# The last chunk's hand-over to the down-projection: one split earlier, one load earlier, and the last two groups crossed by tiles

## What is computed

```python
def conv_ffn(h, w_up, conv_w, conv_b, w_down):
    u = causal_dwconv(h @ w_up, conv_w, conv_b)      # width 3
    gate, val = jnp.split(u, 2, axis=-1)             # 2816 columns each
    return (jax.nn.silu(gate) * val) @ w_down        # 2816 -> 1024

for i in range(2):
    ...                                              # mixer, cross-attention, output projection
    x = x + conv_ffn(rms_norm(x, ffn_norm[i]), ffn_w_up[i], ffn_conv_w[i], ffn_conv_b[i], ffn_w_down[i])
```

## Time and profile before

| | before |
|---|---|
| runs, us | 2585.62, 2587.39, 2590.01 (median 2587.39) |
| the profiled execution, us | 2585.62 |
| its span from first to last instruction, us | 2583.8 |
| PE busy | 2489.5 us, 96% |
| DVE, ACT, POOL busy | 60%, 38%, 8% |
| mean granted TensorE clock | 0.986 of full |

### The profile page before, as it was taken

The page is one execution under the profiler, slowest core; times in us unless marked ns, Lnnn a source line. Parts: engine busy times, 40 slices in busy tenths (PEclk is TensorE's granted clock), DMA queues, the critical chain, the costliest instruction groups (busy, mean ns, idle before and its releaser), DMA issues. The chain is left out here.

```text
span 2583.8 us, 32258 instructions
## 1 busy us (share of the span) xinstructions
PE 2489.5 (96%) x11964; PEld 2109.8 (82%) x11964; DVE 1539.9 (60%) x2562; ACT 992.0 (38%) x2000; POOL 196.0 (8%) x269
## 2 busy tenths in 40 slices
PE   7999979999999999998999999998999999999998
PEld 7998767888888878787889889887888888887886
DVE  4432464489999863433553562464779998984332
ACT  6433443344444432423334432333444444443221
POOL 1010020000000000001211021113000000000000
PEclk9999988999999999999999999999999999999999
DMA  4320112222222246442102011212622222226442
GB/s 145 99 75 21 50 66 62 86 67 94 78 90 82 74 163 225 157 146 73 52 17 78 34 33 45 55 33 79 197 86 82 90 82 75 89 90 242 170 159 81
DMA packets 207475, 240.41 MB, mean 93 GB/s; under 512 B 36776, under 2 KB 140184, under 8 KB 207320
## 3 DMA queue, kind: packets, MB, share of 16 engines
q1 hardware_dynamic: 203160, 238.34, 27.8%
q10 hardware_dynamic: 4160, 0.02, 0.1%
HBM read 189.24 MB, written 49.09 MB: 92 GB/s over the span
## 5 line engine op out<-in xcount | busy, mean ns | idle before, releaser
L53 PE MATMUL psum<-f_T_lo,f_up_hi 128*128 128x512 f32 x1024 | 400.7, 391 | 0.0
L52 PE MATMUL psum<-f_T_lo,f_up_hi 128*128 128x512 f32 x704 | 277.8, 395 | 20.9 <-DVE f_up_lo L523 19.4
L54 PE MATMUL psum<-f_T_lo,f_up_lo 128*128 128x512 f32 x704 | 276.1, 392 | 0.0
L518 DVE TENSOR_TENSOR f_T_lo<-h_room_hi,f_T_lo 128x2048 fp32r<-128x2048 f32 x44 | 100.8, 2292 | 261.6 <-ACT f_T_lo L341 261.6
L52 PE MATMUL psum<-w_hi,hT_hi 128*128 128x512 f32 x576 | 229.5, 398 | 4.1 <-DVE w_lo L1224 2.4
L54 PE MATMUL psum<-w_hi,hT_lo 128*128 128x512 f32 x576 | 226.5, 393 | 0.0
L53 PEld LDWEIGHTS psum<-f_T_lo,f_up_hi 128*128 128x128 f32 x1024 | 193.8, 189 | 39.9
L53 PE MATMUL psum<-w_lo,hT_hi 128*128 128x512 f32 x576 | 226.3, 393 | 0.0
L341 ACT ACTIVATE f_T_lo<-h_room_hi 128x2048 fp32r<-128x2048 f32 x44 | 84.3, 1916 | 307.3 <-PE psum L54 276.9
L52 PEld LDWEIGHTS psum<-f_T_lo,f_up_hi 128*128 128x128 f32 x704 | 133.5, 190 | 51.3 <-DVE f_up_lo L523 21.9
L54 PEld LDWEIGHTS psum<-f_T_lo,f_up_lo 128*128 128x128 f32 x704 | 133.4, 189 | 28.0
(11 more groups left out here) (367 smaller groups left out, 5629.2 us busy)
## 6 DMA issues: line engine op xcount, KB each, us to landing
raw<-in_ffn_w_up_dram SPq DMA_DIRECT2D x88, 512.0 KB, 4.6
h_room_hi<-in_ffn_w_down_dram SPq DMA_DIRECT2D x88, 512.0 KB, 4.6
activations<-f_act SPq DMA_DIRECT2D x44, 512.0 KB, 2.6
h_room_lo<-activations SPq DMA_DIRECT2D x44, 512.0 KB, 6.0
w_raw<-in_b_w_in_dram SPq DMA_DIRECT2D x18, 1024.0 KB, 6.2
x_between<-XY SPq DMA_DIRECT2D x16, 512.0 KB, 5.1
XY<-x_between SPq DMA_DIRECT2D x4, 2048.0 KB, 12.1
w_raw<-in_a_w_in_dram SPq DMA_DIRECT2D x8, 768.0 KB, 5.8
```

The costliest lines, as they stand in the source:

```text
L52: nc.tensor.matmul(out, lhs_hi, rhs_hi, start=start, stop=False)
L53: nc.tensor.matmul(out, lhs_hi, rhs_lo, start=False, stop=False)
L54: return nc.tensor.matmul(out, lhs_lo, rhs_hi, start=False, stop=stop)
L518: nc.vector.tensor_tensor(w_lo[s], w_raw[s], w_hi[s].bitcast(F32), ALU.subtract).then_inc(b_split, 1)
```

## The change

Three places in `ffn_phase`, so each acts in f0 and in f1:

- SP issues `load_down(2)` right behind `load_down(1)`, ahead of the store of the last chunk; `begin`'s loads come behind `load_down(3)`, and lose a wait of their own.
- In the last chunk DVE's `low_down(0)` and `low_act(0)` move from behind C21 to behind U3, the step that takes the fourth product, P7; U4, C22 and C21 now come after them.
- PE waits for group 20 alone, multiplies its tiles 6 and 7, and only then waits for group 21; tiles 4 and 5 take both groups as before, tiles 6 and 7 group 21 alone.

```diff
             load_down(1)
+            load_down(2)
             store_act(FC - 1)
-            if begin:
-                sp.wait_ge(op_split, operand(FC - 1, S4))
-                begin.load(sp)
-            for n in range(2, LAST + 1):
+            for n in range(3, LAST + 1):
                 load_down(n)
+                if begin and n == 3:
+                    begin.load(sp)
...
                 mix_step(c, U3)
+                if not more:
+                    low_down(0)
+                    low_act(0)
                 if more:
...
                 mix_step(c, C21)
                 if more:
                     low(c + 1, L22)
-                else:
-                    low_down(0)
-                    low_act(0)
...
+            wait_split(LAST - 1)
+            for t in (6, 7):
+                for half in range(2):
+                    down(LAST - 1, t, half, False, False)
             wait_split(LAST)
             for t in range(4, TT):
                 for half in range(2):
-                    down(LAST - 1, t, half, False, False)
+                    if t < 6:
+                        down(LAST - 1, t, half, False, False)
                     down(LAST, t, half, False, True).then_inc(out_done, 1)
```

## The result

The changed kernel takes 2567.18 us in the median of four executions, beside 2586.51 us for the kernel before on the same chip: a ratio of 0.992, 95% interval 0.990 to 0.994. The forecast was 2566.0 us, its range 2561.5 to 2571.5. In two later comparisons the ratio was 0.990 (0.989 to 0.991) and 0.991 (0.990 to 0.993). The profiled execution takes 2567.03 us, its span is 2565.3 (2583.8 before), PE is busy 2485.6 us, 97%.

What follows compares the result with a forecast made beforehand. PE, busy 96%, bounds the kernel; gains come from its waits and slow-clock matmuls. Terms 9.4 - 0.6 + 7.7 + 4.8 give 21.3 us, so 2566.0 us against the median of 2587.39, range 2561.5 to 2571.5.

Steps and rivals of the forecast that it cites:

- The crossing: End of each phase, groups 20 and 21: half of group 20 fills PE's wait, gaining 7.7 us in f1, 4.8 in f0.
- Group 0's split earlier: Start of each phase: group 0's wait goes, so group 1 starts 0.88 us earlier in f0, 1.11 in f1.
- Load 2 earlier: Group 2 follows group 1 without a wait; with the earlier split, 6.4 us gained in f0 and 3.0 in f1.
- Load 2 behind load 1: Load 2, queued behind load 1, delays it by 0.3 us per phase, costing 0.6 us in all.
- the upper bound: Most that load 2 was expected to delay load 1: 0.9 us from the rows, 1.1 allowed, per phase.
- lower bound: Least that load 2 could delay load 1: 0, if the queue serves in order.
- The start from one sample: Group 1 in f0 can't start before 951.23, leaving a new pause of about 0.8 us before it.
- The slow clock: The 1.72 us lost to the lower clock behind f0's group 2 goes along with its wait.
- The rival: A slow stretch arises in f0's middle, costing 1.7 us, 2567.7; chance 0.12 together with load 1 held up.
- The sum: Both phases together: 9.4 - 0.6 + 7.7 + 4.8 = 21.3 us gained; within 2.5 us of 2566, chance 0.68.
- the forecast's three signs for being wrong: Load 1's weights reach ACT over 7 us after issue; PE waits over 1 us for group 21; clock falls mid-f0.

Runs made afterwards that it cites:

- no_cross: The changed kernel with the last two groups multiplied as before, without the crossing; 2577.05 us, ratio 0.995 to the kernel before.
- the held one: The changed kernel with SP issuing group 2's load only after group 1's three DMAs have landed; 2564.76 and 2564.07 us in two runs.
- split_late: The changed kernel with group 0's split put back behind C21; 2563.93 us, ratio 0.990 to the kernel before.
- after_third: The changed kernel unedited, run a third time; 2566.49 us, ratio 0.991 to the kernel before.

## Why the prediction held, and the step that was off

- **The crossing** (12.5 us): right, nearly to the tenth against the trace it was worked out from. Behind group 19 f1 gains 7.7 us and f0 4.8, with or without the other parts. Against the second trace of the kernel before, whose clock fell for longer behind group 20 (33.19 us instead of 31.80), f0 gains 6.2, against no_cross 5.7 and f1 7.1. The norm takes back what was reckoned: waits of 0.78 and 0.82 us where 0.9 and 1.2 stood. Group 21 makes no wait, where 0.1 stood.
- **Group 0's split earlier** (part 1, 0.9 and 1.1 us): not borne out. Its wait goes, but behind load 2 group 1's split ends too late for that to reach group 1; with it and without it the two distances are the same within their scatter. What no_cross gains in them, 8.0 us against the first trace of the kernel before and 9.8 against the second, is then nearly all part 2's; 8.8 stood for both parts less the hold-up.
- **Load 2 earlier** (part 2): group 2 follows without a wait in every trace that has the edit, as said.
- **Load 2 behind load 1** (0.6 us): this term was mis-sized. It measured 1.0 us in f0 and 0.6 in f1, 1.6 in all, near the upper bound in f0. Changed kernel against the held one alone (three traces, two) it is 0.7 and 1.3. From the Trainium skill's rule ("DMA: Bandwidth & Descriptors", Queues, rings and completion order), that each DMA engine consumes descriptors in ring order, the prediction concluded a cost of 0 as its lower bound; the runs show that this does not follow. The same section says that a later descriptor may finish its write before an earlier one, so order of consumption does not promise an unhindered finish. What the two loads compete for, no run here shows.
- **The start from one sample:** group 1 was put at 951.23 from the 6.07 us of one load. Load 1 alone scatters by 0.9 us in f0, and that one was its fastest split. This adds 0.5 us.
- **The slow clock** (1.72 us in f0): half right. It no longer falls behind group 2, but the pause before group 1, 2 us instead of 0.8 to 1.1, brought it back in two of four traces, this one among them, for 1.6 us. The rival looked for it in the middle of f0, where it did fall in most traces and cost 0 to 0.8 us, since a wait of 1.55 us stands behind it.
- **The sum** for the two stretches was 21.3 us; the first pair of traces gives 18.9, with 257.85 us in f0 where 255.3 would have been right and 240.62 in f1 where 240.8. The missing 2.6 us in f0 are the 1.0 by which the split came later than forecast and the 1.6 of clock. Over two traces of before and three of after it is 19.5. The whole time agreed within 1.2 us, in part by luck: the gain was 2 us short (19.3 of 21.4), and the median of the kernel before came out 0.9 lower, 2586.51 for 2587.39. Of the forecast's three signs for being wrong, the first came (7.39 us to ACT's start), the third in other traces, and neither was large enough.
- **Open:** the ratios of the three comparisons amount to 20, 26 and 23 us, while the two stretches give 19.5, which lies in the interval of the first and the third and under that of the second. The traces show how much the rest scatters: outside the two distances the span is 2062.4 to 2067.9 us, in no order of the kernels. The stretch from the span's start to f0's last product, which apart from its last chunk is the same in every kernel, takes 934.0 us (split_late) to 942.5 (after_third), and in all fourteen traces it is the longer the lower its granted clock is (0.983 to 0.974 over the first 930 us). Whether the comparisons' medians differ by this chance, no trace shows. Why the hold-up reaches f0's weights in each trace and f1's in one of six is open too.

## What to carry to other kernels

A wait that is removed from the first of a chain of groups can go to the next one whose operands are bound by something else; look there first (here the load of group 1), and shorten that load by taking out of it what can be loaded earlier. Price a load by several samples, and count the load queued right behind it. Work that is left over from the last group but one, put in front of the last group's wait, gave its full length here where nothing else waits (f1), and the low clock behind that wait as well; in f0 the chain behind it took 2 us of that back.

## What was not expected of the hardware

- A load that was queued behind another one slowed it: 1.6 us to the landing of its last DMA, 1.0 us of about 12 to the end of the split in f0, and again about 1 us of 5 to 6 to ACT's start when the load in front was two DMAs of 512 KB.
- The granted clock after a pause of about 2 us differs between executions: 0.62 and 0.66 in two traces (1.97 and 2.05 us), 1.00 in two others (1.87 and 1.99). Before groups 0, 1 and 2 it stayed at full after 1.83 us or less and fell after 2.65 and more; before group 20, after 5.52 us, it fell each of six times; in f0's middle, after 3.6 us, in twelve of fourteen traces. A fall cost 1.4 to 1.6 us in groups 1 and 2, 1.4 to 2.8 in groups 20 and 21 before the change, and 0 to 0.8 in the middle, where another wait follows.
